# The first attention's rotated scores: queries and their remainders stacked on 128 partitions

## The chip, the cores and the metric

One core of a Trainium2 chip runs the whole program in one launch. The time is that of the device in microseconds, from an execution's start to its end. An engine's name stands as in the profile: PE is TensorE (its matmuls), PEld its loads of stationary operands, DVE is VectorE, ACT is ScalarE, POOL is GpSimd, SP the engine that issues most DMAs (SPq).

## The reference, cut to what matters

The program is a stack of three blocks (a Hyena and mLSTM mixer, latent attention, a second attention with a state-space branch and a mixture of experts). Only the latent attention (`mla_mixer`) is touched: 512 latent tokens ask, 768 tokens (256 of context, 512 latent) answer, in 8 heads. A head's query and key have 128 channels without position and 64 that are rotated; the 64 of the key are one set for all heads.

```python
MLA_HEADS = 8; MLA_NOPE = 128; MLA_ROPE = 64; MLA_V = 128

def apply_rope2d(x, cos, sin):
    xa = x.reshape(x.shape[:-1] + (2, ROPE_AXIS))
    x1, x2 = jnp.split(xa, 2, axis=-1)
    ...
    return jnp.concatenate([x1 * c - x2 * s, x2 * c + x1 * s], axis=-1).reshape(x.shape)

def mla_kv(kv_a, k_r, kv_norm, w_ukv, rope):
    ...
    k = jnp.concatenate([k_n, jnp.broadcast_to(k_r, (B, L, MLA_HEADS, MLA_ROPE))], axis=-1)
    return k, v

def attend(q, k, v):
    s = jnp.einsum('bqhd,bkhd->bhqk', q, k).astype(F32) * MLA_SCALE
    p = jax.nn.softmax(s, axis=-1).astype(v.dtype)
    return jnp.einsum('bhqk,bkhd->bqhd', p, v)
```

## The kernel before

All products of PE are made of rounded operands (`fp32r`). So that float32's accuracy is kept, an operand x is held as a pair: a rounded part (high) and the rounded rest x - high (low). ACT writes the high part with a copy, DVE the low part with a subtraction. A product of two pairs is three products that add up in PSUM: high by high, low by high, high by low (`three_passes`, lines 301 to 306; the first of them stands in the profile as L304, then L305 and L306). Work is cut into stages; each is a block in which every engine has its own list, with semaphores between them, and all engines meet at its end.

`mla` (line 2445) makes the latent attention in these stages: projections down, norms, the queries' rotated part (`qr_plain`, 4 tiles of 128 channels by 512 tokens; a tile holds two heads, the even one on partitions 0 to 63, the odd one on 64 to 127), the queries' and keys' other parts, then the two stages that matter here.

**The rotation stage** is `rotate_and_values` (line 2338), 1469.7 to 1501.7 us. For each of 4 query tiles and the keys' latent part, DVE multiplies by cosines (L2413), adds the partner that PE permuted (L2366, L2415, L2416), ACT copies the sum to the high part (L2387), and DVE subtracts for the low part (L2404), one tile later. Between them stands the splitting of the value weights (L2381, L2409). Then PE makes the values in 12 tiles of 6 products of 512 columns, ACT and DVE split each (L2396, L2430). PSUM has room for 4 of these tiles, so PE's fifth waits until DVE is through with the rotation and with the first tile. SP issues only the two loads of the value weights, the second after the first half's weights are split. The key's rotated channels lie twice, on partitions 0 to 63 and 64 to 127 (the weights are doubled on the host), so that either head of a tile finds them beside its own.

**The attention stage** is `attention` (line 2121), called in line 2487 with 8 heads and `ahead` 1, 1501.8 to 1664 us. A unit is one head and 128 queries, so there are 32. Each of the four engines' lists runs over the units in this order:

- PE: scores of unit u+1, half of the values of a pair of earlier units (9 products of 256 columns, from u=2), then it waits that unit u's probabilities are normalised (`normed`) and that the one PSUM room for transposes is free (`t_kept`), and transposes unit u's probabilities (6 of 128 by 128, L2195).
- ACT: high part of the transposed unit u-1 (L2217), at even u from 4 on the high part of an output (L2222), then the exponentials of unit u+1 (L2210).
- DVE: waits for the exponentials of unit u, reciprocal (L2263), normalises (L2264), low part of unit u-1 (L2250), at even u from 4 on the low part of an output (L2256), then the maximum of unit u+1's scores (L2244, L2245).

The scores of a unit go segment by segment (256 context keys, then 512 latent ones). In each segment three products have the 128 unrotated channels as rows, and three have the 64 rotated ones, of the partitions where the head lies:

```python
    def rope_half(h):
        return slice(64 * (h % 2), 64 * (h % 2) + 64)
```

The second block's attention (32 units, 2398 to 2515 us) uses the same function with one set of 64 rows and 512 columns.

Of the kernel before, what the change touches and what calls it, by code (L numbers as in the profile page):

```python
# [24 lines left out]
F32 = mybir.dt.float32  # L25
# [3 lines left out]
ALU = mybir.AluOpType  # L29
AX = mybir.AxisListType  # L30

P = 128
# [268 lines left out]
def three_passes(k, out, stationary, moving, start, stop, **more):  # L301

    (sh, sl), (mh, ml) = stationary, moving
    k.nc.tensor.matmul(out, sh, mh, start=start, stop=False, **more)  # L304
    k.nc.tensor.matmul(out, sh, ml, start=False, stop=False, **more)  # L305
    return k.nc.tensor.matmul(out, sl, mh, start=False, stop=stop, **more)  # L306

# [1813 lines left out]
def attention(k, heads, key_segs, queries_of, keys_of, value_of, out_rows, dst_of, scale, rooms):  # L2121
# [16 lines left out]
    def scores(u):  # L2138
        return rooms.score_banks[u % n_scores]
# [198 lines left out]
def rotate_and_values(k, parts, cos, sin, scratch, plain, names, v, x, at):  # L2338
# [8 lines left out]
    landed, w_high, w_ready, product, cut, taken = (k.sem(s) for s in ("landed", "w_high", "w_ready", "product", "cut", "taken"))  # L2347
    tiles = [(half, j) for half in range(2) for j in range(n_tiles)]

# [3 lines left out]
    with k.block() as block:  # L2353
        @block.sync
        def _(sp):
            for half, name in enumerate(names):
                if half:
                    sp.wait_ge(w_ready, kt)
                sp.dma_start(raw, k.dram[name].rearrange("p (k n) -> p k n", n=width)).then_inc(landed, 16)

        @block.tensor
        def _(pe):
            for n, (y, *out) in enumerate(parts):
# [13 lines left out]
        def _(act):  # L2377
# [21 lines left out]
        def _(dve):  # L2399
            chain = Chain(dve, k.sem("chain"))  # L2400

            def split_off(n, y, high, high_plain, low):
                dve.wait_ge(rounded, n + 1)
                return nc.vector.tensor_tensor(low, y, high_plain, ALU.subtract)  # L2404
# [6 lines left out]
            todo = list(plain) + list(parts)  # L2411
            for n, (y, *out) in enumerate(parts):
# [5 lines left out]
                for m in range(len(plain) if n == 0 else 0):  # L2418
                    split_off(m, *todo[m])
                if n:  # L2420
                    split_off(len(plain) + n - 1, *parts[n - 1])
                if n == 2:
                    weights(0)
            split_off(len(todo) - 1, *parts[-1]).then_inc(left, 1)
# [20 lines left out]
def mla(k, norm):  # L2445
# [9 lines left out]
    qr, at = Pair(k, at, at + 4 * LAT, 4, LAT, CTX), at + 8 * LAT  # L2455
# [11 lines left out]
    rotate_and_values(k, [(qr_plain[:, n, :], qr.high[:, n, :], qr.high_plain[:, n, :], qr.low[:, n, :]) for n in range(4)]  # L2467
                 + [(low[:, 5, CTX:T], kr.high[:, 0, CTX:T], kr.high_plain[:, 0, CTX:T], kr.low[:, 0, CTX:T])],
                 cos, sin, scratch, [(low[:, 5, 0:CTX], kr.high[:, 0, 0:CTX], kr.high_plain[:, 0, 0:CTX], kr.low[:, 0, 0:CTX])],
                      ("mla_w_v0", "mla_w_v1"), v, kva, H_LOW_AT)  # L2470

    def rope_half(h):
        return slice(64 * (h % 2), 64 * (h % 2) + 64)

    def queries_of(h, a):
        nope = qn.tokens(h, CTX + a * P, CTX + (a + 1) * P)
        return nope, [part[rope_half(h), :] for part in qr.tokens(h // 2, CTX + a * P, CTX + (a + 1) * P)]

    def keys_of(h, t0, t1):
        return kn.tokens(h, t0, t1), [part[rope_half(h), :] for part in kr.tokens(0, t0, t1)]  # L2480
# [6 lines left out]
    attention(k, MLA_HEADS, SEGS, queries_of, keys_of, lambda h, b: v.tokens(b, h * P, (h + 1) * P), lambda h: slice(0, P),  # L2487
# [546 lines left out]
def second_mixer(k, norm):  # L3034
# [29 lines left out]
    def half(h):  # L3064
        return slice(64 * (h % 2), 64 * (h % 2) + 64)

    def dst_of(h, part):
# [5 lines left out]
              lambda h, a: ([part[half(h), :] for part in q_pair.tokens(h // 2, CTX + a * P, CTX + (a + 1) * P)],),  # L3073
              lambda h, t0, t1: ([part[half(h), :] for part in k_pair.tokens(h // 4, t0, t1)],),
# [736 lines left out]
```

## Time and profile before

| | |
|---|---|
| three runs | 3197.97, 3209.40, 3214.88 us (median 3209.4) |
| profiled execution, from its first to its last instruction | 3207.9 us |
| that execution's own time | not listed apart; of the three runs, 3209.40 is the nearest to its span, 1.5 us above |
| PE busy, by its modelled ends | 2924.0 us (91%) |
| DVE, ACT, POOL busy | 1710.8, 1207.4, 166.6 us |
| mean granted clock of PE | 0.957 of full |

One execution is profiled. Every instruction has a start and a duration; the starts of PE's products are what it keeps to, while their ends are modelled, so neighbours overlap and the pace of PE is the distance between starts. "Idle before" and "<-" tell how long an engine stood before an instruction, and whose instruction released it. PEclk is the clock that PE was granted, 1.00 being 2.4 GHz and 0.50 being 1.2 GHz.

### The profile page before, as it was taken

The numbers are of one execution on the slowest core, as the hardware profiler recorded it, in microseconds if no ns is written. First come the engines' busy times: TensorE is split into PE (matmuls) and PEld (weight loads), VectorE is DVE, ScalarE is ACT, GpSimd is POOL, SyncE is SP. The second block draws the span as 40 slices with busy tenths as digits, with TensorE's granted clock in tenths as the row PEclk, the third lists the DMA queues.
The fourth block names the chain that finished last, engine by engine and source line by source line (L and its number), as shares of the span: only waits on it lengthen the run. The fifth ranks groups of instructions, "written<-read, shape, count | busy, mean of one in ns | idle before, by whom it ended". The sixth has DMA issues, their size and how long they took to land. (4 is left out here: it accounts for less than half of the span.)

```text
span 3207.9 us, 37971 instructions
## 1 busy us (share of the span) xinstructions
PE 2924.0 (91%) x14246; PEld 2331.5 (73%) x14246; DVE 1710.8 (53%) x2417; ACT 1207.4 (38%) x1619; POOL 166.6 (5%) x127
## 2 busy tenths in 40 slices
PE   7999989799999899898999999989878899899996
PEld 3774777678888798675777887867745677777775
DVE  7535323634767453435654433352366563788886
ACT  2320222424232242423334433244424432477774
POOL 0000001100011000000000000000000100122220
PEclk9999999899999999998999999999979998999998
DMA  8300110021345142110012221212200023799996
GB/s 367 131 20 13 53 53 2 27 92 56 122 147 174 66 151 98 53 37 27 1 34 85 94 102 66 95 62 85 79 8 1 1 66 122 277 360 363 353 347 238
DMA packets 76008, 362.79 MB, mean 113 GB/s; under 512 B 13170, under 2 KB 17043, under 8 KB 50292
## 3 DMA queue, kind: packets, MB, share of 16 engines
q1 hardware_dynamic: 62356, 327.66, 28.5%
q0 software_dynamic: 13536, 33.58, 3.1%
q8 instruction: 73, 1.20, 0.1%
q14 instruction: 43, 0.35, 0.0%
HBM read 360.67 MB, written 16.25 MB: 117 GB/s over the span
## 5 line engine op out<-in xcount | busy, mean ns | idle before, releaser
L304 PE MATMUL ps<-rounded,rounded 128*128 128x512 f32 (+3 forms) x3700 | 1381.6, 373 | 150.7 <-DVE rounded L2250 23.8
L305 PE MATMUL ps<-rounded,rounded 128*128 128x512 f32 (+3 forms) x3700 | 1340.8, 362 | 0.0
L306 PE MATMUL ps<-rounded,rounded 128*128 128x512 f32 (+3 forms) x3700 | 1338.9, 362 | 0.0
L304 PEld LDWEIGHTS ps<-rounded,rounded 128*128 128x128 f32 (+1 forms) x3700 | 707.8, 191 | 337.6 <-issue 112.4
L306 PEld LDWEIGHTS ps<-rounded,rounded 128*128 128x128 f32 (+1 forms) x3700 | 709.1, 192 | 107.9
L305 PEld LDWEIGHTS ps<-rounded,rounded 128*128 128x128 f32 (+1 forms) x3700 | 710.5, 192 | 95.3
L283 DVE TENSOR_TENSOR rounded<-work,rounded 128x1024 fp32r<-128x1024 f32 (+3 forms) x224 | 306.4, 1370 | 818.6 <-ACT rounded L279 818.4
L279 ACT CAST rounded<-work 128x1024 fp32r<-128x1024 f32 (+3 forms) x224 | 260.8, 1166 | 707.2 <-PE ps L306 612.1
L3562 DVE TENSOR_TENSOR rounded<-work,rounded 128x2048 fp32r<-128x2048 f32 x138 | 309.7, 2286 | 71.9 <-ACT rounded L3390 71.9
L3390 ACT CAST rounded<-work 128x2048 fp32r<-128x2048 f32 x138 | 259.1, 1913 | 77.9 <-PE ps L306 77.9
L290 PE MATMUL ps<-cst 128*128 128x256 f32 x566 | 147.3, 417 | 35.3 <-PEq L170 35.3
L290 PEld LDWEIGHTS ps<-cst 128*128 128x128 f32 x566 | 117.0, 212 | 59.9 <-issue 42.6
L279 ACT ACT_TABLE_LOAD x34 | 43.6, 1283 | 205.4 <-PE ps L306 196.3
L478 DVE SCALAR_TENSOR_TENSOR work<-work,silu_c 128x256 f32<-128x256 f32 x224 | 103.7, 484 | 14.1 <-DMA work<-in_ada_w 8.3
L2830 POOL TENSOR_TENSOR h<-work,row 128x2048 f32<-128x2048 f32 x2 | 8.2, 4100 | 1470.9 <-DVE h L2904 1470.9
L1005 DVE SCALAR_TENSOR_TENSOR work<-ps,vec,work 128x255 f32 (+4 forms) x116 | 72.5, 653 | 19.5 <-ACT work L975 13.6
L1083 ACT ACTIVATE work<-work 128x768 f32<-128x768 f32 (+1 forms) x44 | 32.5, 739 | 128.2 <-DVE work L1118 128.2
L2250 DVE TENSOR_TENSOR rounded<-ps,rounded 128x768 fp32r<-128x768 f32 (+1 forms) x64 | 52.3, 818 | 41.1 <-ACT rounded L2217 41.1
L1396 PE MATMUL ps<-work 128*128 128x512 f32 x160 | 71.6, 607 | 0.0
L3274 POOL DMA_INDIRECT y_rows<-h,whole x23 | 51.6, 2243 | 345.5 <-ACT h L3428 345.5
L2244 DVE TENSOR_REDUCE row<-ps 128x1 f32<-128x768 f32 (+1 forms) x64 | 52.5, 820 | 26.0 <-PE ps L306 25.8
L2210 ACT ACTIVATE x<-ps,row 128x768 f32<-128x768 f32 x32 | 28.9, 902 | 95.9 <-DVE row L2245 95.9
(487 smaller groups left out, 2483.8 us busy)
## 6 DMA issues: line engine op xcount, KB each, us to landing
work<-in_moe SPq DMA_DIRECT2D x138, 1024.0 KB, 7.4
work<-in_ffn_up SPq DMA_DIRECT2D x44, 1024.0 KB, 4.8
work<-in_ffn_down SPq DMA_DIRECT2D x66, 512.0 KB, 3.4
work<-in_ada_w SPq DMA_DIRECT2D x12, 2048.0 KB, 12.9
work<-in_ada_w POOLq DMA_DIRECT2D x48, 512.0 KB, 4.0
work<-in_w_out SPq DMA_DIRECT2D x16, 512.0 KB, 3.5
work<-in_w_gates SPq DMA_DIRECT2D x16, 512.0 KB, 3.5
work<-in_w_in_hy SPq DMA_DIRECT2D x12, 512.0 KB, 3.5
```

What stands on the lines that cost most here:

```text
L279: self.k.nc.scalar.copy(self.parts[s][0], self.raw[s]).then_inc(self.rounded[s], 1)
L283: self.k.nc.vector.tensor_tensor(self.parts[s][1], self.raw[s], self.high_plain[s], ALU.subtract).then_inc(self.ready[s], 1)
L290: k.nc.tensor.matmul(k.bank(bank, 2 * P), k.const("ident"), k.cst[:, 0:2 * P], start=True, stop=True)
L304: k.nc.tensor.matmul(out, sh, mh, start=start, stop=False, **more)
L305: k.nc.tensor.matmul(out, sh, ml, start=False, stop=False, **more)
L306: return k.nc.tensor.matmul(out, sl, mh, start=False, stop=stop, **more)
L478: done = self.k.nc.vector.scalar_tensor_tensor(out=total, in0=tile, scalar=by, in1=total, op0=ALU.mult, op1=ALU.add)
L1005: nc.vector.scalar_tensor_tensor(out=out, in0=k.pair(p)[:, lo + o:hi + o], scalar=k.col(conv_w, n + tiles * (o + taps // 2)), in1=out, op0 ...
L1396: last = nc.tensor.matmul(bank(group, part), tab[part][:, a, n * P:(n + 1) * P], src[:, a, :], start=a == 0, stop=a == count - 1)
L2244: chain.link(nc.vector.tensor_reduce(stats[:, b, 0:1], scores(u), AX.X, ALU.max))
L3390: nc.scalar.copy(ring.parts[:, c % ring.SPLIT, 0, :], ring.raw[c % ring.RAW]).then_inc(ring.rounded, 1)
L3562: V.tensor_tensor(ring.parts[:, s, 1, :], ring.raw[c % ring.RAW], ring.plain[:, s, 0, :], ALU.subtract).then_inc(ring.ready, 1)
```

## The change

A tile's high and low parts of the rotated queries no longer lie in two tiles each with two heads. Each head gets a tile of its own, `stacked` (the same 8 by 512 words as before), with the high part on one half of the partitions and the low part on the other. One product with the keys' high part, doubled as it is, then gives high by high plus low by high; a second one with the keys' low part gives high by low, for which that low part is zero on partitions 64 to 127. An even head's high part and an odd head's low part are written in place; the other two are written to a spare tile (in `x`) and are brought to the other half of the partitions by DMAs, two for each query tile. ACT makes two copies of 64 partitions for a query tile and DVE two subtractions. POOL zeroes the keys' lower half. The even head's stack is high over low, the odd head's is high on partitions 0 to 63 as well.

In the attention the caller now gives the list of products (`products_of`), and all of them are issued from line 2172 of the changed program. The second attention issues the same three products as before. The diff, without the second attention's lines and the new arguments:

```diff
+def passes(stationary, moving):
+    (sh, sl), (mh, ml) = stationary, moving
+    return [(sh, mh), (sh, ml), (sl, mh)]
...
@@ attention
-                    queries, keys = queries_of(h, a), keys_of(h, t0, t0 + n)
-                    for i, (one, other) in enumerate(zip(queries, keys)):
-                        last = three_passes(k, scores(u)[:, t0 - lo:t0 - lo + n], one, other, i == 0, i == len(keys) - 1)
+                    products = products_of(h, a, t0, t0 + n)
+                    for i, (queries, keys) in enumerate(products):
+                        last = nc.tensor.matmul(scores(u)[:, t0 - lo:t0 - lo + n], queries, keys, start=i == 0,
+                                                stop=i == len(products) - 1)
...
@@ rotate_and_values
+    upper, lower = slice(0, 64), slice(64, 128)
+    wholes = list(queries) + [key[:, CTX:T]]
...
+            def move(n):
+                sp.wait_ge(halved, n + 1)
+                sp.dma_start(stacked_plain[lower, 2 * n], spare_plain[upper, pieces(n)]).then_inc(moved, 16)
+                sp.dma_start(stacked_plain[upper, 2 * n + 1], spare_plain[lower, pieces(n)]).then_inc(moved, 16)
+
             for half, name in enumerate(names):
                 if half:
                     sp.wait_ge(w_ready, kt)
                 sp.dma_start(raw, k.dram[name].rearrange("p (k n) -> p k n", n=width)).then_inc(landed, 16)
+                for n in range(2 * half, 2 * half + 2):
+                    move(n)
+            sp.wait_ge(moved, 16 * 2 * len(queries))
+
+        @block.gpsimd
+        def _(pool):
+            pool.memset(kr.low_plain[lower, 0, :], 0.0).then_inc(zeroed, 1)
+            pool.wait_ge(zeroed, 1)
...
-            for y, high, high_plain, low in plain:
-                nc.scalar.copy(high, y).then_inc(rounded, 1)
-            for n, (y, high, high_plain, low) in enumerate(parts):
+            nc.scalar.copy(kr.high[:, 0, 0:CTX], key[:, 0:CTX]).then_inc(rounded, 1)
+            for n, y in enumerate(wholes):
                 act.wait_ge(summed, n + 1)
-                nc.scalar.copy(high, y).then_inc(rounded, 1)
+                if n < len(queries):
+                    nc.scalar.copy(spare[lower, pieces(n)], in_two(y)[lower])
+                    nc.scalar.copy(stacked[upper, 2 * n], in_two(y)[upper]).then_inc(rounded, 1)
+                else:
+                    nc.scalar.copy(kr.high[:, 0, CTX:T], y).then_inc(rounded, 1)
...
-            def split_off(n, y, high, high_plain, low):
-                dve.wait_ge(rounded, n + 1)
-                return nc.vector.tensor_tensor(low, y, high_plain, ALU.subtract)
+            def query_low(n):
+                y = in_two(queries[n])
+                dve.wait_ge(rounded, n + 2)
+                nc.vector.tensor_tensor(spare[upper, pieces(n)], y[upper], stacked_plain[upper, 2 * n], ALU.subtract)
+                nc.vector.tensor_tensor(stacked[lower, 2 * n + 1], y[lower], spare_plain[lower, pieces(n)], ALU.subtract).then_inc(halved, 1)
...
@@ mla
-    qr, at = Pair(k, at, at + 4 * LAT, 4, LAT, CTX), at + 8 * LAT
+    qr, at = k.rounded(at, 8, LAT), at + 8 * LAT
...
+    def products_of(h, a, t0, t1):
+        both = qr[:, h, a * P:(a + 1) * P]
+        return passes(qn.tokens(h, CTX + a * P, CTX + (a + 1) * P), kn.tokens(h, t0, t1)) + [(both, part) for part in kr.tokens(0, t0, t1)]
```

On PE, at the attention's first unit, before. A row is a product; `rounded_37632` and `rounded_38400` are the rotated keys' high and low parts, `rounded_34816` and `rounded_36864` the rotated queries' two:

```order
L304 MATMUL ps<-rounded_18432_49,rounded_28672_6904 128x256
L305 MATMUL ps<-rounded_24576_6903,rounded_28672_6904 128x256
L306 MATMUL ps<-rounded_18432_49,rounded_32768_6905 128x256
L304 MATMUL ps<-rounded_37632_6908,rounded_34816_6906 128x256
L305 MATMUL ps<-rounded_38400_6909,rounded_34816_6906 128x256
L306 MATMUL ps<-rounded_37632_6908,rounded_36864_6907 128x256
L304 MATMUL ps<-rounded_18432_49,rounded_28672_6904 128x512
```

And the same place after the change, where `rounded_36864` is the stack:

```order
L2172 MATMUL ps<-rounded_18432_49,rounded_28672_6904 128x256
L2172 MATMUL ps<-rounded_24576_6903,rounded_28672_6904 128x256
L2172 MATMUL ps<-rounded_18432_49,rounded_32768_6905 128x256
L2172 MATMUL ps<-rounded_37632_6907,rounded_36864_6906 128x256
L2172 MATMUL ps<-rounded_38400_6908,rounded_36864_6906 128x256
L2172 MATMUL ps<-rounded_18432_49,rounded_28672_6904 128x512
```

The third product of the rotated channels is gone, in this segment and in the next; the program's PE list is 64 rows shorter, 6689 where it was 6753.

On DVE, in the rotation stage, the first query tile's subtraction and the second tile's work, after the change (before, one row of 128x512, L2404, stands in the place of L2445 and L2446):

```order
L2454 TENSOR_TENSOR work<-work 128x512
L2456 TENSOR_TENSOR work<-ps,work 128x512
L2457 TENSOR_TENSOR work<-work 128x512
L2445 TENSOR_TENSOR rounded_6144_8119<-work,rounded_36864_6906 64x2x256
L2446 TENSOR_TENSOR rounded_36864_6906<-work,rounded_6144_8119 64x512
```

DVE's list has 4 rows more. On SP the stage now issues, in this order:

```order
L2384 DMA h<-in_mla_w_v 128x1024
L2378 DMA rounded_36864_6906<-rounded_6144_8119 64x2x256
L2379 DMA rounded_36864_6906<-rounded_6144_8119 64x2x256
L2378 DMA rounded_36864_6906<-rounded_6144_8119 64x2x256
L2379 DMA rounded_36864_6906<-rounded_6144_8119 64x2x256
L2384 DMA h<-in_mla_w_v 128x1024
```

Four more moves follow, and then the wait for all eight; before, the two loads stood alone.

## Rows read from the trace of the kernel before

**Rows 1.** The page: its first line.

```profile
span 3207.9 us, 37971 instructions
```

**Rows 2.** PE's products in order of time, one unit's scores: start, length, engine, operation.

```profile
1577.68 0.28 PE L306 MATMUL ps<-rounded,rounded 128*128 128x256 f32 x1
1577.89 0.38 PE L304 MATMUL ps<-rounded,rounded 64*128 64x256 f32 x1
1578.11 0.28 PE L305 MATMUL ps<-rounded,rounded 64*128 64x256 f32 x1
1578.23 0.28 PE L306 MATMUL ps<-rounded,rounded 64*128 64x256 f32 x1
1578.44 0.50 PE L304 MATMUL ps<-rounded,rounded 128*128 128x512 f32 x1
1578.78 0.40 PE L305 MATMUL ps<-rounded,rounded 128*128 128x512 f32 x1
1579.02 0.40 PE L306 MATMUL ps<-rounded,rounded 128*128 128x512 f32 x1
1579.34 0.49 PE L304 MATMUL ps<-rounded,rounded 64*128 64x512 f32 x1
```

**Rows 3.** DVE's work of one unit, in order of time, ACT's rows left out.

```profile
1575.73 0.96 DVE L2244 TENSOR_REDUCE row<-ps 128x1 f32<-128x768 f32 x1 [0.58 <-PE ps L306]
...
1577.93 0.16 DVE L2263 RECIPROCAL row<-row 128x1 f32<-128x1 f32 x1 [1.06 <-ACT x L2210]
1578.13 0.75 DVE L2264 TENSOR_SCALAR x<-x,row 128x768 f32<-128x768 f32 x1
...
1578.80 0.94 DVE L2250 TENSOR_TENSOR rounded<-ps,rounded 128x768 fp32r<-128x768 f32 x1
1579.66 0.41 DVE L2256 TENSOR_TENSOR rounded<-ps,rounded 128x256 fp32r<-128x256 f32 x1
1580.34 0.96 DVE L2244 TENSOR_REDUCE row<-ps 128x1 f32<-128x768 f32 x1 [0.27 <-PE ps L306]
```

**Rows 4.** Waits from 1560 to 1650 us: total us, times, longest.

```profile
DVE row L2244 <- PE ps L306: 8.5, 20, 0.6
```

**Rows 5.** Order of time: the attention's first product, DVE's fifth and last maximum.

```profile
1501.83 0.35 PE L304 MATMUL ps<-rounded,rounded 128*128 128x256 f32 x1 [1.67 <-PEq L170]
...
1529.65 0.96 DVE L2244 TENSOR_REDUCE row<-ps 128x1 f32<-128x768 f32 x1 [0.90 <-PE ps L306]
...
1654.05 0.96 DVE L2244 TENSOR_REDUCE row<-ps 128x1 f32<-128x768 f32 x1 [0.27 <-PE ps L306]
```

**Rows 6.** Stretches: length, busy us (instructions) of each engine, PEclk, DMA, GB/s.

```profile
1479.00:1482.00 3.00, 2.98 (x7) 2.41 (x8) 2.90 (x5) 0.35 (x1) 0.00 (x0) 0.50 0.47 135
1482.00:1486.00 4.00, 4.00 (x18) 3.06 (x17) 3.67 (x6) 1.08 (x3) 0.00 (x0) 1.00 0.07 30
1502.50:1526.00 23.50, 23.50 (x67) 15.93 (x68) 8.91 (x16) 5.87 (x11) 0.00 (x0) 0.50 0.00 0
2398.50:2402.50 4.00, 4.00 (x9) 2.76 (x9) 1.86 (x6) 2.17 (x4) 0.00 (x0) 0.50 0.02 6
2415.00:2510.00 95.00, 75.04 (x426) 55.71 (x424) 61.64 (x153) 38.76 (x97) 0.00 (x0) 1.00 0.00 1
```

**Rows 7.** The rotation stage in order of time: DVE's last subtractions, PE's fifth value tile.

```profile
1484.43 1.34 DVE L2404 TENSOR_TENSOR rounded<-work,rounded 128x512 fp32r<-128x512 f32 x2
...
1487.17 0.50 PE L304 MATMUL ps<-rounded,rounded 128*128 128x512 f32 x1 [1.05 <-DVE rounded L2430]
```

**Rows 8.** Groups by line, whole span: subtractions of 64 and 128 partitions, a memset.

```profile
L2256 DVE TENSOR_TENSOR rounded<-ps,rounded 64x256 fp32r<-64x256 f32 x16 | 6.7, 417 | 1.9 <-ACT rounded L2222 1.7
L2256 DVE TENSOR_TENSOR rounded<-ps,rounded 128x256 fp32r<-128x256 f32 x16 | 6.7, 416 | 2.6 <-ACT rounded L2222 2.6
L1880 POOL MEMSET work<- 64x768 f32 x1 | 0.7, 735 | 0.0
```

**Rows 9.** DMA issues: KB each, us from issue to landing.

```profile
work<-in_mla_w_kn SPq DMA_DIRECT2D x8, 128.0 KB, 2.0
```

More of the change, by code:

```diff
@@ L2118, in __init__, with attention @@
         self.score_banks, self.turn_banks, self.out_banks, self.ahead = score_banks, turn_banks, out_banks, ahead
-def attention(k, heads, key_segs, queries_of, keys_of, value_of, out_rows, dst_of, scale, rooms):
+def attention(k, heads, key_segs, products_of, value_of, out_rows, dst_of, scale, rooms):
     nc = k.nc
@@ L2335, in _, with rotate_and_values @@
             in_turns(dve, turns, turn)
-def rotate_and_values(k, parts, cos, sin, scratch, plain, names, v, x, at):
+def rotate_and_values(k, queries, stacked, spare, key, kr, cos, sin, scratch, names, v, x, at):
     nc = k.nc
@@ L2347, in rotate_and_values, with in_two, pieces @@
     landed, w_high, w_ready, product, cut, taken = (k.sem(s) for s in ("landed", "w_high", "w_ready", "product", "cut", "taken"))
+    halved, moved, zeroed = (k.sem(s) for s in ("halved", "moved", "zeroed"))
     tiles = [(half, j) for half in range(2) for j in range(n_tiles)]
+    upper, lower = slice(0, 64), slice(64, 128)
+    wholes = list(queries) + [key[:, CTX:T]]
+    stacked, spare_plain = stacked.rearrange("p n (a t) -> p n a t", t=CTX), spare.bitcast(F32)
+    stacked_plain = stacked.bitcast(F32)
+    def in_two(y):
+        return y.rearrange("p (a t) -> p a t", t=CTX)
+    def pieces(n):
+        return slice(2 * n, 2 * n + 2)
     def sums(m):
@@ L2409, in weights @@
                     nc.vector.tensor_tensor(w.low[:, kk, :], raw[:, kk, :], w.high_plain[:, kk, :], ALU.subtract).then_inc(w_ready, 1)
-            todo = list(plain) + list(parts)
-            for n, (y, *out) in enumerate(parts):
+            for n, y in enumerate(wholes):
                 chain.link(nc.vector.tensor_tensor(scratch, y, cos, ALU.mult))
@@ L2417, in _ @@
                 dve.wait_ge(summed, n + 1)
[L2418 to L2421, printed above, removed]
+                if n == 0:
+                    key_low(0, CTX, 1)
+                else:
+                    query_low(n - 1)
                 if n == 2:
                     weights(0)
-            split_off(len(todo) - 1, *parts[-1]).then_inc(left, 1)
+            key_low(CTX, T, len(wholes) + 1).then_inc(left, 1)
             for m, (half, j) in enumerate(tiles):
@@ L2466, in mla @@
     project_split(k, "mla_w_kn", kn, SEGS, 2, kva)
[L2467 to L2480, printed above, removed]
+    rotate_and_values(k, [qr_plain[:, n, :] for n in range(4)], qr, k.rounded(X_AT, DT, T)[:, :, 0:CTX], low[:, 5, :], kr,
+                      cos, sin, scratch, ("mla_w_v0", "mla_w_v1"), v, kva, H_LOW_AT)
+    def products_of(h, a, t0, t1):
+        both = qr[:, h, a * P:(a + 1) * P]
+        return passes(qn.tokens(h, CTX + a * P, CTX + (a + 1) * P), kn.tokens(h, t0, t1)) + [(both, part) for part in kr.tokens(0, t0, t1)]
     def dst_of(h, half):
@@ L2486, in mla @@
     rooms = AttentionRooms(probs, turned, [k.pair(0), k.pair(1)], [k.pair(2)], [k.bank(6), k.bank(7)], 1)
-    attention(k, MLA_HEADS, SEGS, queries_of, keys_of, lambda h, b: v.tokens(b, h * P, (h + 1) * P), lambda h: slice(0, P),
+    attention(k, MLA_HEADS, SEGS, products_of, lambda h, b: v.tokens(b, h * P, (h + 1) * P), lambda h: slice(0, P),
               dst_of, MLA_SCALE, rooms)
@@ L3072, in second_mixer @@
     attention(k, SSD_HEADS, SEG_LAT,
-              lambda h, a: ([part[half(h), :] for part in q_pair.tokens(h // 2, CTX + a * P, CTX + (a + 1) * P)],),
-              lambda h, t0, t1: ([part[half(h), :] for part in k_pair.tokens(h // 4, t0, t1)],),
+              lambda h, a, t0, t1: passes([part[half(h), :] for part in q_pair.tokens(h // 2, CTX + a * P, CTX + (a + 1) * P)],
+                                          [part[half(h), :] for part in k_pair.tokens(h // 4, t0, t1)]),
               lambda h, b: v_pair.tokens(b, (h // 4) * P, (h // 4) * P + P), half, dst_of, 0.125, rooms)
```

5 lines of the change are left out of this document (4 added, 1 removed).

## The prediction

> **What bounds the kernel now.** First the page's first line, to have the span that every saving is taken from: 3207.9 us [rows 1]. The change touches two stages, so I read those two and not the averages over the program. In the attention I follow PE's starts in order of time [rows 2], to see what one product and one passage between 128 and 64 rows take. Then DVE's list in the same unit [rows 3] and the waits [rows 4]: the reader is to see that DVE stands idle before each maximum until PE has finished the scores, 8.5 us in 20 units, 0.425 us a unit. PE waits for nobody in a unit. So PE sets the pace, by a small margin. The pace is (1654.05 - 1529.65) / 27 = 4.607 us a unit [rows 5]. Last the granted clock [rows 6]: for the attention's first 23.5 us it is 0.50, the 1.2 GHz level. In the rotation stage DVE sets the pace, and PE's fifth value tile waits for it [rows 7].
>
> **PE's saving per unit.** Removed are one 64-row product of 256 and one of 512 columns. Inside a triple, starts lie 0.12 us apart at 256 columns (1578.11 to 1578.23) and 0.24 at 512 (1578.78 to 1579.02) [rows 2]: 0.36 us. At a passage the distance grows: 1577.68 to 1577.89 is 0.21 for 0.12, and the first 64-row product to the next is 0.22 for 0.12, together 0.19. Back to 128 rows it is 0.21 for 0.12 and 0.34 for 0.24, again 0.19. The next passage begins alike (1579.02 to 1579.34, 0.32 for 0.24). A unit has four, 0.76 us in all. With every product on 128 rows I take all four away. PE then needs 4.61 - 0.36 - 0.76 = 3.49 us a unit.
>
> The Trainium skill, in "TensorE: Matmul & The Clock Gate", section "Why this matters for your kernels", says that a product of few rows lasts as long as one of 128; by that rule alone only the 0.36 us would go. "TensorEngine Tiling (Array Packing)", section "Key Properties", of the same skill says that a change of tiling mode drains TensorE, which would give the other 0.76 us too. The trace has both: equal pace inside the triples, and longer steps at the passages only.
>
> **What is late next.** DVE's loop cannot follow. From a maximum to the reciprocal are 2.20 us (1575.73 to 1577.93, 1.06 of it waiting for ACT's exponentials), 0.20 to the normalising, 0.67 to the subtraction L2250, and 0.86 until L2256 starts behind it [rows 3]. That is 3.93 us for a unit without L2256, and 3.93 + 0.41 - 0.08 = 4.26 with one, since neighbours without a wait overlap by 0.08 (0.94 long, 0.86 apart). From the fifth maximum to the last there are 14 units with it and 13 without: 14 x 4.26 + 13 x 3.93 = 110.7 us where 124.4 stand now. Gain 13.7 us. If the overlap does not occur, DVE gives back just its idle time, 27 x 0.425 = 11.5 us. I take 13.0, nearer to the first, because L2250 and L2256 show the overlap at waits already met. PE will idle some 0.6 us a unit before the transposes, which wait for L2250; of PE's 1.12 us a unit about half is lost there.
>
> **The slow beginning.** Here the change pays more, since PE at 1.2 GHz is far from DVE's limit. At that level a 512-column product takes 0.43 us: 7 of 128 rows in 3.0 us, 9 of 64 rows in 4.0 us [rows 6]; so rows make no difference in length and 64-row products in a row have no gaps. By columns I estimate 0.21 for 256. PE starts at 1501.83 [rows 5]. Unit 0's ten products take about 3.2 us, to 1505.0, and unit 1's 3.2 more, to 1508.2. DVE's first maximum starts at 1505.1, its second 2.20 + 0.20 + 0.67 later, at 1508.2. If the clock is up again by about then, three loops of 3.93 put the fifth maximum at 1520.0, against 1529.65 now: 9.6 us. If it stays low as now until values are made, a unit takes scores of 3.2 and transposes of 1.2 (twice an estimated 0.6): third maximum 1512.7, fourth 1517.2, then 2.1 of values, transposes and scores, fifth 1522.2: 7.4 us.
>
> Which? In the rotation stage 3 us of 128-row products at the low level were followed by 1.00; 4 us of 64-row products without a gap, in the second attention, were not; and the attention's mixture kept 0.50 for 23.5 us [rows 6]. After the change PE starts with 6 us of 128-row products without a gap. I take the early rise, 9.6 us.
>
> **The rotation stage.** Four query tiles cost DVE one subtraction more each. One of half the partitions takes as long as a whole one (417 and 416 ns for 256 columns [rows 8]), so 512 columns take 0.67 to 0.69 as now (1.34 for two [rows 7]): 4 x 0.69 = 2.8 us. They lie on the path: the values' first subtraction comes after them, and PE's fifth tile waits 1.05 us for it already, which becomes 2.4, since PE's first tile also starts two subtractions, 1.4 us, later. All the tiles behind move back by the whole 2.8. ACT's four extra copies take the same order of time, but ACT waits for DVE's next sum each time: nothing, unless the copies were three times as long. The memset, 0.7 us on POOL [rows 8], runs beside the first multiplication; between nothing and 0.7 us if it holds DVE up, I take 0.2. The eight moves are of 128 KB each. A load of that size lands in 2.0 us [rows 9]; the last two are issued at some 1487, and even at four times that they land by 1495, with the stage ending near 1504. SP's second weight load passes behind four of them, but its semaphore is set after the two subtractions that these wait for, and its data are needed some 8 us later: nothing. Sum of the stage: +3.0 us.
>
> **The sum.** -13.0 - 9.6 + 3.0 = -19.6 us. The profiled execution has a span of 3207.9; its own time is not listed, but a run of 3209.4 lies 1.5 above it and is also the median. I forecast 3209.4 - 19.6 = 3189.8, said as **3190 us**. Everything behind the attention moves up unchanged.
>
> **The rivals.**
>
> *The clock rises late.* For it speaks that it stayed low for 23.5 us. Against it, what stood before the rise in the rotation stage. -13.0 - 7.4 + 3.0 = -17.4: 3192. Chance 0.20.
>
> *The passages stay.* If the longer steps come from the change of operands and not of rows, PE needs 4.25 us a unit and stays the bound: 27 x 0.36 = 9.7, four slow units of 0.64 each 2.6, less 3.0: -9.3, 3200. Against it: 128-row products of different tiles follow each other at the plain pace in the rotation stage. Chance 0.08.
>
> *The rotation stage costs more.* PE's wait of 2.4 us lets the clock fall (it was 0.50 after the longer pause before 1479 [rows 6]); then the next 3 us make 7 products and not 13, 1.4 us. Or the moves hold up the second weight load, for which 2 to 5 us are a bound from a landing of 2.0 [rows 9] for each that stands before it. With 5 more: -14.6, 3195. Chance 0.14.
>
> *Slower.* PE now idles in every unit. If that makes the granted clock fall, a unit needs 3.2 + 1.2 + 1.9 = 6.3 us at 1.2 GHz, PE is dense, and the clock rises again. Spending half of the time at either level gives 5.2 us a unit: 27 x 0.6 = +16, less 7.4 for the beginning, plus 3.0: +12; at three quarters low it would be 5.75 a unit, 27 x 1.14 = +31, then +27: 3236. It decides against the change as soon as more than a third of the units run low. Against it: the second attention keeps 1.00 for 95 us with PE busy 75 of them [rows 6], less than the 85% expected here. Chance 0.04, at about 3225. The Trainium skill, same page on the clock gate, section "A second HAM failure mode: psum-queue depth-cycling", describes short idle times between groups of products that make the clock swing; the second attention's row disagrees.
>
> **How the numbers follow.** The forecast's own case has 0.54. Two in ten may be left out: the low end is the forecast less what the overlap and the memset could add, 1 us, and less some 6 us, as the three runs lie 17 us apart: 3182. The high end takes in the late clock, the costlier rotation and the passages: 3201. Half a per cent, 16 us, is about what a measurement of this kernel can tell from no change; that is 3193.4. Forecast and late clock lie under it by 3.6 and 1.4 us, so faster gets 0.5 of the first's 0.54, 0.14 of the second's 0.20, and 0.05 from the rest, 0.69 together; slower by that much 0.04; the same 0.27.
>
> **What would show it.** Steps right: no 64-row product between 1502 and 1660, starts 0.12 and 0.24 apart through all five; DVE's maximum no longer waits for PE, a unit takes 4.1 us, and PE waits for L2250's successor before the transposes; PEclk is up by about 1508; the rotation stage is 3 us longer. Wrong: steps of 0.2 left inside the scores; maxima still waiting for PE; a PEclk under 1.00 after 1530; DVE or ACT durations changed by the halved partitions; a stage end that waits for SP.

## The result and the profile after

| | before | after |
|---|---|---|
| median of 5 runs each, us | 3214.9 (3198.0 to 3223.9) | 3191.6 (3188.1 to 3202.5) |
| ratio, with its 95% interval | | 0.9938 (0.9912 to 0.9964) |
| profiled execution: span, us | 3207.9 [rows 1] | 3189.8 |
| rotation stage, DVE's first multiplication to the attention's first product | 32.12 | 36.67 |
| attention, first product to the fifth maximum | 27.82 [rows 5] | 16.86 |
| fifth to last maximum, 27 units | 124.40 [rows 5] | 110.52 |
| last maximum to the next stage's first product | 10.48 | 11.32 |

The ratio of 0.9938 is 19.9 us of 3214.9, between 11.6 and 28.3; the two medians of the table lie further apart, 23.3 us, which is inside that interval. The profiled execution's own time is 3191.6 us. The page's first lines:

```profile
span 3189.8 us, 37865 instructions
...
PE 2886.6 (90%) x14182; PEld 2315.8 (73%) x14182; DVE 1710.8 (54%) x2421; ACT 1210.8 (38%) x1623; POOL 167.5 (5%) x128
```

The lines that answer to [rows 5], in order of time:

```profile
1502.55 3.75 PE L2172 MATMUL ps<-rounded,rounded 128*128 128x256 f32 x20 [1.67 <-PEq L170]
...
1519.41 0.95 DVE L2251 TENSOR_REDUCE row<-ps 128x1 f32<-128x768 f32 x1
...
1629.93 0.95 DVE L2251 TENSOR_REDUCE row<-ps 128x1 f32<-128x768 f32 x1
```

No maximum but the very first waits for PE any more. The attention is 162.70 - 138.70 = 24.00 us shorter, the rotation stage 4.55 longer: 19.45 net. The span fell by 18.1. The rest lies in code that the change does not touch: DVE's first multiplication came 3.8 us earlier (1465.88 for 1469.71), and what follows the attention took 5.2 longer. I put neither down to the change: what follows the attention took from 1536.7 to 1553.6 us in the thirteen traces of this document, without a change there, and its mean granted clock was 0.96 in the shortest and 0.95 in the longest.

One unit in order of time, for [rows 2] and [rows 3]; the row with x10 holds a unit's ten score products:

```profile
1576.63 0.95 DVE L2251 TENSOR_REDUCE row<-ps 128x1 f32<-128x768 f32 x1
...
1578.83 0.16 DVE L2270 RECIPROCAL row<-row 128x1 f32<-128x1 f32 x1 [1.06 <-ACT x L2217]
...
1579.70 0.94 DVE L2257 TENSOR_TENSOR rounded<-ps,rounded 128x768 fp32r<-128x768 f32 x1
1580.56 0.41 DVE L2263 TENSOR_TENSOR rounded<-ps,rounded 128x256 fp32r<-128x256 f32 x1
1580.69 0.39 PE L304 MATMUL ps<-rounded,rounded 128*128 128x256 f32 x1 [0.99 <-DVE rounded L2257]
1580.89 0.95 DVE L2251 TENSOR_REDUCE row<-ps 128x1 f32<-128x768 f32 x1
...
1582.44 1.98 PE L2172 MATMUL ps<-rounded,rounded 128*128 128x256 f32 x10
...
1584.25 0.28 PE L304 MATMUL ps<-rounded,rounded 128*128 128x256 f32 x1
...
1584.81 0.95 DVE L2251 TENSOR_REDUCE row<-ps 128x1 f32<-128x768 f32 x1
```

Ten products take 1584.25 - 1582.44 = 1.81 us, against 5 x 0.12 + 5 x 0.24 = 1.80: the longer steps are gone. A maximum comes 4.26 us after the one before where L2263 stands between, and 3.92 where it does not. PE now waits 0.99 us in every second unit, with the clock up: stretches, for [rows 6]:

```profile
1502.50:1526.00 23.50, 18.73 (x123) 16.09 (x124) 14.69 (x28) 10.55 (x19) 0.00 (x0) 1.00 0.01 1
1526.00:1620.00 94.00, 83.15 (x580) 74.55 (x579) 68.00 (x128) 41.89 (x81) 0.00 (x0) 1.00 0.00 1
```

And the waits from 1545 to 1640 us, for [rows 4] (total us, times, longest; the one of 1.9 us stands behind the last maximum, the other eleven are of 0.94 to 1.00):

```profile
DVE row L2270 <- ACT x L2217: 23.3, 22, 1.1
...
PE ps L304 <- DVE rounded L2257: 12.7, 12, 1.9
```

The rotation stage in order of time, for [rows 7]:

```profile
1471.05 0.68 DVE L2445 TENSOR_TENSOR rounded<-work,rounded 64x512 fp32r<-64x512 f32 x1
1471.74 0.69 DVE L2446 TENSOR_TENSOR rounded<-work,rounded 64x512 fp32r<-64x512 f32 x1
1472.46 0.69 DVE L2454 TENSOR_TENSOR work<-work 128x512 f32<-128x512 f32 x1
...
1486.54 0.50 PE L304 MATMUL ps<-rounded,rounded 128*128 128x512 f32 x1 [2.06 <-DVE rounded L2471]
```

In a query tile a subtraction of half the partitions takes 0.68 to 0.69 us and there are two. PE's fifth value tile waits 2.06 us for 1.05 before.

### The profile page after: what moved, and what is told of

Same layout as the page of the kernel before. It is cut to its first block and busy times, and to the rows that moved or that the text cites. A ratio compares the mean times of both kernels' runs of the same rounds, so it can differ in the third digit from the quotient of the medians.

```text
span 3189.8 us, 37865 instructions
## 1 busy us (share of the span) xinstructions
PE 2886.6 (90%) x14182; PEld 2315.8 (73%) x14182; DVE 1710.8 (54%) x2421; ACT 1210.8 (38%) x1623; POOL 167.5 (5%) x128
## 5 line engine op out<-in xcount | busy, mean ns | idle before, releaser
L304 PE MATMUL ps<-rounded,rounded 128*128 128x512 f32 (+1 forms) x3540 | 1301.8, 368 | 161.3 <-DVE rounded L2257 38.5
L305 PE MATMUL ps<-rounded,rounded 128*128 128x512 f32 (+1 forms) x3540 | 1279.4, 361 | 0.0
L306 PE MATMUL ps<-rounded,rounded 128*128 128x512 f32 (+1 forms) x3540 | 1278.2, 361 | 0.0
L304 PEld LDWEIGHTS ps<-rounded,rounded 128*128 128x128 f32 x3540 | 675.2, 191 | 314.2 <-issue 74.3
L306 PEld LDWEIGHTS ps<-rounded,rounded 128*128 128x128 f32 x3540 | 674.9, 191 | 102.4
L305 PEld LDWEIGHTS ps<-rounded,rounded 128*128 128x128 f32 x3540 | 676.5, 191 | 95.5
L2172 PE MATMUL ps<-rounded,rounded 128*128 128x256 f32 (+2 forms) x416 | 96.7, 372 | 5.1 <-PEq L170 5.1
L1011 DVE SCALAR_TENSOR_TENSOR work<-ps,vec,work 128x255 f32 (+4 forms) x116 | 72.5, 653 | 19.5 <-ACT work L981 13.6
L2172 PEld LDWEIGHTS ps<-rounded,rounded 128*128 128x128 f32 (+1 forms) x416 | 64.1, 193 | 18.7 <-issue 12.4
L2257 DVE TENSOR_TENSOR rounded<-ps,rounded 128x768 fp32r<-128x768 f32 (+1 forms) x64 | 52.3, 817 | 40.3 <-ACT rounded L2224 40.3
```

What stands on the lines that cost most here:

```text
L1011: nc.vector.scalar_tensor_tensor(out=out, in0=k.pair(p)[:, lo + o:hi + o], scalar=k.col(conv_w, n + tiles * (o + taps // 2)), in1=out, op0 ...
L2172: last = nc.tensor.matmul(scores(u)[:, t0 - lo:t0 - lo + n], queries, keys, start=i == 0, stop=i == len(products) - 1)
```

## The experiments

In each, the pace is the distance from the fifth to the last maximum of the scores divided by 27.

**1. Rows alone: all twelve products stay, the rotated ones take 128 rows.**

```diff
# in the kernel before
     def rope_half(h):
-        return slice(64 * (h % 2), 64 * (h % 2) + 64)
+        return slice(0, 128)
```

> The kernel before, its three rotated products per segment kept, but each on all 128 rows of the tile; the rotation stage is the old one. (What it leaves out: the separation of the two heads of a tile, so each head's rotated score also has its neighbour's.) Theory (passages between 64 and 128 rows cost PE 0.19 us each, and DVE's loop binds at 4.10 us a unit): steps of 0.12 and 0.24 us throughout, PE needs 3.85 us a unit, DVE's maxima no longer wait for PE, pace 4.10 us, the same as with the change although no product is removed; the attention from its first product to the last maximum 127 to 131 us for 152.2 before; the rotation stage 32 us as before. Whole: about 23 us less than before, 0.993. Rival (the number of products counts): pace 4.61, whole 1.000.

Measured: 3187.9 us against 3210.7, ratio 0.9924 (0.9905 to 0.9943). The pace is (1633.10 - 1522.40) / 27 = 4.10 us, and from the first product to the last maximum are 128.3 us. The rotation stage, the old one, took 32.98 us for the 32 expected, which comes up again below. PE's scores in one unit, in order of time:

```profile
1582.20 0.40 PE L305 MATMUL ps<-rounded,rounded 128*128 128x512 f32 x1
1582.44 0.39 PE L306 MATMUL ps<-rounded,rounded 128*128 128x512 f32 x1
1582.66 0.39 PE L304 MATMUL ps<-rounded,rounded 128*128 128x512 f32 x1
...
1583.80 0.39 PE L304 MATMUL ps<-rounded,rounded 128*128 128x256 f32 x1 [0.29 <-DVE rounded L2250]
```

From L306 at 1582.44 to L304 at 1582.66 the operands change from the unrotated to the rotated ones: 0.22 us, the plain step, where [rows 2] had 0.32 at the same place (1579.02 to 1579.34). So the long steps belong to the change of rows, not to the change of operands. That one line of code brings the pace all the way to DVE's limit, and PE already waits for DVE. The clock stayed up from the start, which I come back to:

```profile
1502.50:1526.00 23.50, 18.77 (x118) 15.63 (x116) 14.24 (x26) 9.98 (x17) 0.00 (x0) 1.00 0.00 1
```

**2. One product fewer, rows left at 64.**

```diff
# in the kernel before, for the second operand set
-                        last = three_passes(k, scores(u)[...], one, other, i == 0, i == len(keys) - 1)
+                            for j in range(2):
+                                last = nc.tensor.matmul(scores(u)[...], one[0], other[j], start=False, stop=j == 1)
```

> The kernel before, with only two rotated products per segment (the product of the keys' high part with the queries' remainders is left out), both on 64 rows; the old rotation stage. Theory: the four passages stay, so PE needs 4.25 us a unit and stays the bound: pace 4.25, DVE still waits some 0.1 us for PE, steps of 0.21 and 0.34 at the passages stay. Gain 27 x 0.36 + about 3 in the slow beginning = 12 to 13 us, 0.996. Rival (products count, not passages): pace 4.10 and as much gain as with the change less its rotation stage, 0.992.

Measured: 3199.3 us, ratio 0.9965 (0.9951 to 0.998). The pace is (1641.61 - 1526.67) / 27 = 4.257. PE's scores in one unit:

```profile
1579.72 0.28 PE L306 MATMUL ps<-rounded,rounded 128*128 128x256 f32 x1
1579.92 0.50 PE L2170 MATMUL ps<-rounded,rounded 64*128 64x256 f32 x2
1580.36 0.50 PE L304 MATMUL ps<-rounded,rounded 128*128 128x512 f32 x1
1580.69 0.39 PE L305 MATMUL ps<-rounded,rounded 128*128 128x512 f32 x1
1580.92 0.40 PE L306 MATMUL ps<-rounded,rounded 128*128 128x512 f32 x1
1581.25 0.73 PE L2170 MATMUL ps<-rounded,rounded 64*128 64x512 f32 x2
```

The steps at a change of rows are still there: 0.20 for 0.12 (1579.72 to 1579.92), 0.33 for 0.24 (1580.36 to 1580.69, and 1580.92 to 1581.25). The lost product is worth its own 0.36 us a unit and no more. PE stays the bound, if narrowly: DVE's maximum still waits, 2.2 us in 9 times from 1545 to 1625 us.

**3. A third product of 128 rows put back into the changed kernel.**

```diff
-    return passes(...) + [(both, part) for part in kr.tokens(0, t0, t1)]
+    return passes(...) + [(both, part) for part in kr.tokens(0, t0, t1)] + [(both, kr.low[:, 0, t0:t1])]
```

> The changed kernel with a third product of 128 rows per segment, a repetition of the one with the keys' low part (which then counts twice in the scores). Theory: PE needs 3.49 + 0.36 = 3.85 us a unit, still under DVE's 4.10; pace 4.10, PE's wait for L2257 shrinks by 0.36 a unit, the time as with the change within 1.5 us (0.994 of before). Rival (each product is worth its length): 32 x 0.36 = 11.5 us slower than with the change, 0.997 of before.

Measured: 3190.6 us, ratio 0.994 (0.9921 to 0.9959), beside 0.9938 for the change. The pace is (1637.02 - 1526.31) / 27 = 4.10. The scores, and PE's waits from 1545 to 1625 us:

```profile
1581.25 2.33 PE L2172 MATMUL ps<-rounded,rounded 128*128 128x256 f32 x12
```

```profile
PE ps L304 <- DVE rounded L2257: 2.9, 10, 0.3
```

The longest group of products grew by 2.33 - 1.98 = 0.35 us, and each wait for DVE, one in two units, shrank from 1.0 to 0.3. Once all products have 128 rows, the removed one is worth nothing: PE has the time to spare.

**4. DVE's limit lifted: the maxima are taken with the scores two units ahead.** DVE's wait for ACT's exponentials (1.06 us a unit) is what makes its loop long. Here PE and ACT work two units ahead, DVE raises one ahead.

```diff
-            for u in range(ahead):
+            for u in range(rooms.raise_ahead):
                 raise_(u)
...
-                if u + ahead < n_units:
-                    raise_(u + ahead)
+                if u + rooms.raise_ahead < n_units:
+                    raise_(u + rooms.raise_ahead)
...
-    rooms = AttentionRooms(probs, turned, ..., [k.bank(6), k.bank(7)], 1)
+    rooms = AttentionRooms(probs, turned, ..., [k.bank(6), k.bank(7)], 2, raise_ahead=1)
```

> The changed kernel, with PE's scores and DVE's maxima two units ahead in the first attention, and ACT's exponentials one as they are. Theory (DVE's 1.06 us of waiting for ACT inside its loop is what holds the pace at 4.10): that wait goes, DVE's own loop is about 3.1 us, PE's list of 3.5 us becomes the bound; pace 3.5 to 3.6 us, the attention 15 to 17 us shorter than with the change, 0.989 of before. Rival (another chain binds, through the one room for transposes or ACT): pace 3.8 to 4.1, gain under 8 us.

Measured: 3183.4 us, ratio 0.9908 (0.9888 to 0.9928). The pace is (1619.46 - 1520.14) / 27 = 3.68, the attention 138.7 - 126.9 = 11.8 us shorter than after the change. Both expectations missed: it lies between the 15 to 17 us of the theory and the rival's 8. From the first product to the last maximum 16.1 us went (127.4 to 111.3), but from there to the next stage it takes 15.67 us for 11.32, since the maxima run a unit further ahead of the rest. The waits from 1545 to 1625 us:

```profile
ACT rounded L2225 <- PE ps L2203: 40.5, 22, 1.9
DVE rounded L2258 <- ACT rounded L2225: 13.6, 22, 0.7
...
PE ps L304 <- DVE rounded L2258: 3.4, 11, 1.9
```

```profile
1573.39 1.98 PE L2173 MATMUL ps<-rounded,rounded 128*128 128x256 f32 x10
...
1573.67 0.80 ACT L2225 CAST rounded<-ps 128x768 fp32r<-128x768 f32 x1 [1.91 <-PE ps L2203]
...
1574.50 0.96 DVE L2258 TENSOR_TENSOR rounded<-ps,rounded 128x768 fp32r<-128x768 f32 x1 [0.68 <-ACT rounded L2225]
...
1576.85 0.60 PE L2173 MATMUL ps<-rounded,rounded 128*128 128x256 f32 x3
```

DVE no longer waits for exponentials. The unit from 1573.39 to 1576.85 is PE's list without a wait, 3.46 us: the forecast's estimate was 3.49. The next unit takes 3.88 (the scores behind it start at 1580.73): in every second unit PE still waits, by the trace 0.15 us, by the starts 0.42 (the 1.9 stands behind the last maximum). The transposes, ACT's high part and DVE's low part stand in one chain, and the values wait for its end.

**5. The same edit in the kernel before**, to see whether it needs the change.

> The kernel before, with scores and maxima two units ahead, exponentials one. Theory (before the change PE is the bound, and DVE's wait for ACT lies in its slack): pace 4.6 us a unit as before, time 1.000 of before within 0.1%. Rival (DVE's loop mattered before too): pace 4.2 to 4.4, 0.996. The 64-row products are all there, so the clock should fall in the attention's first us, as in the three traces with such products so far.

Measured: 3216.1 us, ratio 1.0012 (0.9993 to 1.0032). No difference. The clock fell 1.2 us after the attention's first product, as expected, and was up again at some 1538, later than in any other trace; whether this edit has a part in that is not shown. Once it is up, maxima lie 4.61 us apart (1636.40 to 1641.01), as before. PE is the bound there, and DVE, waiting less for ACT, waits more for PE; from 1560 to 1640 us:

```profile
DVE row L2245 <- PE ps L306: 12.2, 17, 0.9
```

**6 and 7. Both kernels profiled once more**, for what of the 24 us one profile gives by chance.

> The kernel before once more, for its trace alone. If the slow beginning of the attention (clock at 0.50 for over 20 us) belongs to the 64-row products, it is there again, and the attention takes 150 to 153 us to its last maximum. If it was chance, the clock is up within 5 us, and the attention takes 143 to 145.

> The changed kernel once more, for its trace alone: the attention's pace 4.10 us a unit and no more than 5 us at 0.50 at its beginning, 127 to 129 us to its last maximum; the rotation stage 35 to 37 us, with the clock's fall in it there or not. If the high clock from the beginning was chance, a stretch at 0.50 of more than 5 us stands in it this time.

Before, again:

```profile
1502.50:1526.00 23.50, 22.89 (x98) 15.88 (x98) 11.70 (x21) 7.12 (x13) 0.00 (x0) 0.78 0.00 0
```

After, again:

```profile
1502.50:1526.00 23.50, 17.75 (x110) 14.84 (x109) 13.80 (x25) 9.96 (x16) 0.00 (x0) 1.00 0.00 1
```

From the first product to the last maximum the kernel before took 147.0 us this time (1501.79 to 1648.79), which fell between the two expectations, against 152.2 in the first trace. The clock was up again by some 1513. After took 127.3 (127.4 in the first). From the first product to the fifth maximum before took 22.6 us and after 16.86, so the change is worth 5.7 us there on this pair and 11.0 on the first: half of the larger number is that one trace of before. The rotation stage: 32.1 before, 36.15 after, +4.05. With the rotation stage, the attention and its end the second pair gives 190.75 - 175.38 = 15.4 us, the first 194.82 - 175.37 = 19.5. The two executions as a whole took 3201.0 and 3199.3 us, only 1.8 apart, because what follows took 12.2 us longer after (1551.0 for 1538.8, mean granted clock 0.95 for 0.96): a single execution of each does not show a change of this size.

**8. Keeping PE's clock up in the rotation stage**: ten keep-running rounds before the fifth value tile.

```diff
             for m, (half, j) in enumerate(tiles):
+                if m == 4:
+                    keep_running(k, 10, 1)
```

> The changed kernel with ten products of the identity (256 columns each, to a PSUM bank that is done with) before PE's fifth value tile, where it waits for DVE. Theory (in the rotation stage PE's wait of 2.4 us lets the granted clock fall, and some tiles then run at 1.2 GHz): the clock stays at 1.00 from 1482 to the stage's end, and the stage takes 35 us where the changed kernel took 36.7. Rival (the extra time of the stage is all DVE's subtractions): the stage stays at 36 to 37 us, whatever the clock.

Measured: 3201.2 us in one execution; the stage took 1470.98 to 1507.97, 36.99 us. PEclk was 1.00 from 1486 on, after a stretch at 0.50 before the filler. The ten products stand in the trace as 20, and they outlasted the wait that they were to fill:

```profile
1489.09 4.48 PE L290 MATMUL ps<-cst 128*128 128x256 f32 x20
...
1495.62 0.69 DVE L2473 TENSOR_TENSOR rounded<-ps,rounded 128x512 fp32r<-128x512 f32 x1 [2.26 <-ACT rounded L2434]
```

4.48 us of filler in a wait of 2 us moves the next value tile back, and DVE stands 2.26 us for it. A miss. Nor does it show that the filler kept the clock up: experiment 3 has the same rotation stage without a filler, its clock was at 1.00 from 1490 to the end as well, and it took 35.29 us. There the fifth value tile starts 20.64 us after DVE's first multiplication, here 22.24: the filler cost the 1.6 us. With experiment 4's edit beside it:

> The version with scores and maxima two units ahead, plus the ten identity products in the rotation stage. If both parts hold what their traces showed or promise: the attention 11 to 12 us shorter than with the change alone, the rotation stage 1 to 2 us shorter; 0.990 of before. If the clock's fall costs nothing that lasts, the same time as with two units ahead alone, 0.991.

3177.1 us, ratio 0.9903 (0.9883 to 0.9923), with a stage of 36.96 us, for 36.27 in experiment 4, where 1 to 2 us less than with the change were expected, and an attention of 126.5: not to be told from experiment 4.

**9. Half of the query subtractions given to POOL**, to take the added ones off DVE.

```diff
+            for n in range(len(queries)):
+                pool.wait_ge(rounded, n + 2)
+                nc.gpsimd.tensor_tensor(spare[upper, pieces(n)], in_two(queries[n])[upper], stacked_plain[upper, 2 * n],
+                                        ALU.subtract).then_inc(pooled, 1)
...
-                nc.vector.tensor_tensor(spare[upper, pieces(n)], y[upper], stacked_plain[upper, 2 * n], ALU.subtract)
```

> The changed kernel, with the first of each query tile's two subtractions on POOL instead of DVE. Theory (the rotation stage's extra time is DVE's four subtractions, 0.8 us each with their lost overlap): from DVE's first multiplication to its first value subtraction 16.7 to 17.2 us, as before the change, instead of 19.9; the stage 32 to 33.5 us. Rival (POOL's work slows DVE's beside it, or POOL is late): DVE's multiplications and additions last longer than 0.69 us, and the stage stays over 34.5 us.

Measured: 3204.7 us in one execution; the stage took 1476.57 to 1512.37, 35.80 us. In order of time:

```profile
1481.53 1.25 POOL L2396 TENSOR_TENSOR rounded<-work,rounded 64x512 fp32r<-64x512 f32 x1 [3.49 <-ACT rounded L2426]
...
1481.90 1.43 DVE L2462 TENSOR_TENSOR work<-work 128x512 f32<-128x512 f32 x1
...
1484.81 0.69 DVE L2461 TENSOR_TENSOR work<-ps,work 128x512 f32<-128x512 f32 x1
1485.54 0.96 DVE L2462 TENSOR_TENSOR work<-work 128x512 f32<-128x512 f32 x1
...
1487.86 1.82 POOL L2396 TENSOR_TENSOR rounded<-work,rounded 64x512 fp32r<-64x512 f32 x1 [1.91 <-ACT rounded L2426]
...
1488.47 1.76 DVE L2459 TENSOR_TENSOR work<-work 128x512 f32<-128x512 f32 x1
```

Beside each of POOL's four subtractions one operation of DVE takes longer, 1.43, 0.96, 1.76 and 0.99 us where it takes 0.69 alone. Together these are 2.4 us more for DVE, and the four removed subtractions would have taken 2.8. The operation that reads PSUM (L2461) keeps its 0.69 although POOL works from 1484.69 to 1485.95. From DVE's first multiplication to its first value subtraction are 20.39 us. The first trace of the changed kernel has 19.92, but there the clock was up; the second, with the clock at 0.50 at the stage's beginning as here, has 20.72. So POOL took some 0.3 us off, where 3 were hoped for. The stage stayed over 34.5 us and the rival held. With experiment 4's edit added:

> Two units ahead, and POOL's subtractions. If both hold: attention from first product to the last maximum 111 to 112 us, rotation stage 32 to 33.5; 3.5 us less than two units ahead alone: 0.989 to 0.990 of before.

3179.1 us, ratio 0.9894 (0.9872 to 0.9917); the stage took 34.94 us, 0.35 less than experiment 3's, whose clock was low at the same place. The lowest ratio, but its interval covers the values of experiment 4 alone and of 8: no gain of the whole is shown for POOL.

## Why the prediction was right, step by step

**The size and the sign held**: 19.6 us were forecast, 19.9 measured (3190 us said, 3191.6 found). On the first pair of traces the parts are each near enough that they did not only cancel, but two of them erred by over a microsecond, in opposite directions. That the sum came within half a microsecond is luck all the same: the interval of the measured saving is 17 us wide, and the second pair of traces gives 15.4 us for the stages that the forecast added up to 19.6.

**PE's saving per unit** held in both of its terms. The passages, 0.76 us a unit, went with the rows (experiment 1) and stayed when only the product went (experiment 2); PE's list without a wait is 3.46 us in experiment 4, for 3.49 said. The Trainium skill, "TensorEngine Tiling (Array Packing)", section "Key Properties", says that a change of tiling mode drains the engine, without a price: the price here is 0.08 to 0.10 us at each side, 0.19 for a passage. The rival "the passages stay" falls, and so does the rule taken alone that only the product's own 0.36 us would go.

**The new bound** was DVE, as forecast: pace 4.093, gain 13.9 us for the 13.0 taken and the 13.7 that the full overlap gives. The overlap of neighbouring subtractions is there in all 27 units, which take 4.25 or 4.26 us with L2263 and 3.91 to 3.93 without, where the sum said 4.26 and 3.93. One place was wrong: PE waits before the values (L304 for L2257), not before the transposes. The wait's size was given as 0.6 us a unit on average. The trace lists 0.99 us in every second unit, and by the starts PE loses 4.09 - 3.46 = 0.63 a unit.

**The slow beginning** was the term with the weakest base. I forecast that the clock would start low and be up by 1508, with the fifth maximum 18.2 us after the first product. It never fell, and the fifth maximum came after 16.86. The gain was 11.0 us for 9.6 against the profiled execution. But the second trace of before had only 22.6 us here, so half of the gain depends on which execution was profiled; the sum took one execution's 23.5 us at 0.50 [rows 6] for the kernel's habit. Against the second trace the term is 5.7 us for 9.6, and no run tells what it is on average. The rival of a late rise falls.

**The rotation stage** is the term that was undersized: +3.0 forecast, +4.55 and +4.05 measured. The four subtractions cost DVE 19.92 - 16.72 = 3.2 us, from its first multiplication to its first value subtraction, that is 0.80 each and not 0.69. The lengths were as said, 0.68 and 0.69. The step that failed is to take an operation's length for its price, "512 columns take 0.67 to 0.69 as now". Before, the operation behind L2404 starts 0.61 us after it; now the three starts L2445, L2446, L2454 lie 0.69 and 0.72 apart (1471.05, 1471.74, 1472.46). So the whole cost is 0.69 + 0.72 - 0.61 = 0.80: the overlap with the neighbour is lost. The key's subtraction, also on 64 partitions, keeps it (L2440 from 1468.55, the next from 1468.89, 0.34 apart at a length of 0.42). It works on partitions 0 to 63, L2446 on 64 to 127 between operations that begin at partition 0; that this is the cause was not tested.

The rest comes from the clock and not from the change. In the first trace it is 1.35 us: behind PE's wait of 2.06 us the clock was at 0.50.

```profile
1488.00:1489.00 1.00, 1.00 (x3) 0.77 (x3) 0.28 (x1) 0.57 (x1) 0.00 (x0) 0.50 0.00 0
```

That is the rival "the rotation stage costs more" in its first form, priced at 1.4 us. In the second trace the clock stood at 0.50 at the stage's beginning, and there it was DVE that waited for PE's first permuted product, 1.33 us where the first trace has 0.52:

```profile
1467.09 0.69 DVE L2456 TENSOR_TENSOR work<-ps,work 128x512 f32<-128x512 f32 x1 [0.52 <-PE ps L2399]
```

```profile
1473.07 0.69 DVE L2456 TENSOR_TENSOR work<-ps,work 128x512 f32<-128x512 f32 x1 [1.33 <-PE ps L2399]
```

3.2 + 0.8 = 4.0, of that pair's 4.05. Experiment 1 shows the same with the old stage (32.98 us for 32.12). In experiment 3, which has the changed stage, the clock was low at neither place, and the stage took 35.29 us, 3.17 more than before: that is what the change costs there, for 3.0 said. The clock's fall behind the fifth value tile stands in one of the six traces with stacked queries and no filler, experiment 9's two included; in the other five PE waited 1.3 to 1.6 us there instead of 2.06. Whether the longer wait brought it on is open.

**The parts costed at nothing.** The moves landed in 2.3 us each, and the last was issued at 1485.10, 17 us before the stage's end; SP's second load did not hold up PE. The DMA issues of the stage:

```profile
rounded<-rounded SPq DMA_DIRECT2D x8, 128.0 KB, 2.3
```

The memset (0.73 us from 1466.62) began when DVE's first multiplication had just ended and lay mostly in DVE's wait for PE; the next DVE operation (from 1467.09) took 0.69 as always. So the 0.2 us taken for it was nothing.

**The tail** was forecast unchanged and took 0.8 us more, with the clock at 0.50 from some 1638 on; the second traces have 11.65 for before and 11.91 for after. PE's two waits there are nearly the same (1.21 and 1.88 us before, 1.28 and 1.88 after). The clock fell there in all nine traces whose products have 128 rows and in two of the four others, so whether a part of the 0.8 us is the change's stays open.

**"Slower"**: PE idles a microsecond in every second unit and the clock stayed at 1.00 for the 94 us shown above, with PE busy for 83. The swing that the Trainium skill describes in "TensorE: Matmul & The Clock Gate", section "A second HAM failure mode: psum-queue depth-cycling", did not come in them.

## What to carry to other kernels

Look for the steps between starts and not only for the products: where 64-row and 128-row products alternate, the passage can cost more than the product that one hopes to save, and giving all of them the same rows was worth as much here as the whole change. Then ask what engine is next: two savings on PE of 0.76 and 0.36 us were worth only 0.51 together, because DVE's own loop lay no further than that below PE's; it took a second edit, worth nothing before the first (experiments 4 and 5), to get at the rest. An operation of DVE on half the partitions takes the full time (0.68 us for 0.69), so cutting one tile's work in halves doubles it, and the distance between starts, not the length, is its price. And where the granted clock comes and goes, trace both kernels more than once before a term is taken from a slow stretch.

## What the runs showed of the hardware

**The clock at the attention's start went with the 64-row products.** The same pause of 1.67 us stands before the first product in both kernels. In all four traces in which 64-row products follow (before twice, and experiments 2 and 5) the granted clock fell to 0.50 within 0.6 to 1.2 us of the first product and stayed there for 10 us to more than 30. In none of the nine traces whose products all have 128 rows did it fall there, experiment 1 among them, which has the same twelve products as before and differs in rows alone. Experiment 5, whose attention starts at 1506.0 and whose clock was low from 1507.2 to 1537.9:

```profile
1502.50:1526.00 23.50, 21.83 (x63) 14.03 (x61) 7.78 (x14) 6.13 (x10) 0.00 (x0) 0.60 0.00 0
```

Whether it is the rows or the longer steps at each passage was not separated: no experiment here has one without the other.

**DVE and POOL together**: beside each of POOL's four subtractions one operation of DVE took 1.4 to 2.6 times as long (0.96 to 1.76 us for 0.69); one that reads PSUM took its 0.69. One of POOL's own took 1.82 us, the three others 1.25 to 1.28.
